# Opening loads on two queues, and bias transposes behind the first tile's last pair

## The reference

```
xn   = rms_norm(h, attn_norm_g[layer])          # per token over 1024 channels, times a gain
proj = xn @ w_in[layer]                         # 1024 x 2560: u_ssm, u_g, v_g, q, k, v
y_ssm  = s5_mixer(u_ssm, a_re, a_im, log_dt, b_re, b_im, c_re, c_im, d, w_glu, b_glu)
y_sgu  = spatial_gating(u_g, v_g, ...)
y_diff = diff_attention(q, k, v, ...)
h = h + concat(y_ssm, y_sgu, y_diff) @ w_out[layer]
h = h + conv_gated_mlp(rms_norm(h, ffn_norm_g[layer]), w_up, conv_w, conv_b, w_down)
```

## Time and profile before

| | |
|---|---|
| median of 3 runs | 967.36 us |
| profiled execution, its own time | 965.9 us |
| its span | 964.1 us |
| PE busy | 953.2 us (99%) |
| DVE, ACT, POOL busy | 71%, 59%, 24% |
| granted TensorE clock, mean | 0.999 |

### The profile page before, as it was taken

How to read it: one execution, slowest core, us unless ns; L and a number is a source line. 1 busy time by engine, 2 the same in 40 slices (tenths; PEclk the granted TensorE clock), 3 DMA queues, 4 the chain that set the end, 5 groups by cost and what they waited for, 6 DMA issues and landing times.

```text
span 964.1 us, 15784 instructions
## 1 busy us (share of the span) xinstructions
PE 953.2 (99%) x6119; PEld 837.0 (87%) x6123; DVE 687.8 (71%) x1081; ACT 567.4 (59%) x960; POOL 232.7 (24%) x189
## 2 busy tenths in 40 slices
PE   8999999999999999999999999999999999999997
PEld 6887889999888888899999988999778889888886
DVE  7987868786765877857777754748576755666885
ACT  7977666676855657756666544535454445555733
POOL 6560303535500110302445500021131300000030
PEclk9999999999999999999999999999999999999999
DMA  8642465655664534466665665665544445754452
GB/s 313 213 132 67 156 208 182 190 176 184 194 197 152 182 126 153 133 188 193 181 192 179 195 196 155 215 202 173 165 140 153 153 143 171 200 164 154 153 179 83
DMA packets 48618, 165.96 MB, mean 172 GB/s; under 512 B 6560, under 2 KB 7072, under 8 KB 48544
## 3 DMA queue, kind: packets, MB, share of 16 engines
q1 hardware_dynamic: 48544, 164.95, 54.3%
HBM read 162.83 MB, written 1.05 MB: 170 GB/s over the span
## 4 chain that ended last, share of the span: by engine, by line
PE 87%; ACT 4%; POOL 4%; DVE 3%; issue 1%; DMA 1%; SPq 0%; POOLq 0%; DVEq 0%; ACTq 0%
PE PJ L655 14%; PE PJ L657 13%; PE PJ L656 13%; PE PJ L648 10%; PE PJ L646 10%; PE PJ L647 10%; PE PJ L603 2%; PE PJ L586 2%; PE PJ L593 2%; PE T L1118 1%; ACT sm L1378 1%; ACT whi L1177 1%; PE T L1109 1%; DVE wlo L1874 1%; PE T L1047 1%
## 5 line engine op out<-in xcount | busy, mean ns | idle before, releaser
L1874 DVE TENSOR_TENSOR wlo<-raw,whi 128x1024 fp32r<-128x1024 f32 x294 | 368.7, 1284 | 87.0 <-ACT whi L1177 84.7
L1177 ACT ACTIVATE whi<-raw 128x1024 fp32r<-128x1024 f32 x294 | 301.8, 1059 | 62.9 <-DMA raw<-weights_in 60.6
L646 PE MATMUL PJ<-xthb,whi 128*128 128x256 f32 x832 | 233.7, 281 | 0.0
L648 PE MATMUL PJ<-xthb,wlo 128*128 128x256 f32 x832 | 233.4, 281 | 0.0
L647 PE MATMUL PJ<-xtlb,whi 128*128 128x256 f32 x832 | 232.4, 279 | 0.0
L655 PE MATMUL PJ<-whi,xthb 128*128 128x512 f32 (+1 forms) x424 | 170.9, 403 | 0.4 <-DVE wlo L1874 0.2
L657 PE MATMUL PJ<-whi,xtlb 128*128 128x512 f32 (+1 forms) x424 | 164.0, 387 | 0.0
L656 PE MATMUL PJ<-wlo,xthb 128*128 128x512 f32 (+1 forms) x424 | 163.9, 387 | 0.0
L647 PEld LDWEIGHTS PJ<-xtlb,whi 128*128 128x128 f32 x832 | 157.0, 189 | 0.3
L646 PEld LDWEIGHTS PJ<-xthb,whi 128*128 128x128 f32 x832 | 157.0, 189 | 0.3
L648 PEld LDWEIGHTS PJ<-xthb,wlo 128*128 128x128 f32 x832 | 156.9, 189 | 0.0
(11 more groups left out here) (419 smaller groups left out, 1353.8 us busy)
## 6 DMA issues: line engine op xcount, KB each, us to landing
raw<-weights_in SPq DMA_DIRECT2D x294, 512.0 KB, 3.6
rt<-bmerge_in SPq DMA_DIRECT2D x6, 256.0 KB, 4.2
memx<-mem_in SPq DMA_DIRECT2D x2, 512.0 KB, 4.2
y_out<-xn SPq DMA_DIRECT2D x4, 256.0 KB, 2.3
rowv<-rows_in SPq DMA_DIRECT2D x1, 576.0 KB, 10.4
xres<-x_in SPq DMA_DIRECT2D x2, 256.0 KB, 2.8
xres<-x_in SPq DMA_DIRECT2D x1, 512.0 KB, 6.7
ptmp<-bexp_in SPq DMA_DIRECT2D x2, 256.0 KB, 5.9
```

Source lines behind the costliest of these rows:

```text
L646: pe.matmul(o, a, xh[:, k, :], start=(first and f % 2 == 0), stop=False, skip_group_check=True)
L648: m = pe.matmul(o, b, xh[:, k, :], start=False, stop=last, skip_group_check=True)
L1177: act.activation(whi[:, p % HIGHS, :], raw[:, p % LOADS, :], ACT.Copy).then_inc(hi_ready, 1)
L1874: dve.tensor_tensor(wlo[:, p % LOADS, :], raw[:, p % LOADS, :], whi[:, p % HIGHS, :].bitcast(F32), ALU.subtract).then_inc(lo_ready, 1)
```

## The change

ACT issues two DMAs as its first instructions: the left half of tile 0's rows and weight pair 0. SP starts with the right half of tile 0's rows, then par and the identity, then pairs 1 and 2, tile 1's rows, pair 3, bex, pair 4 and the rest as before. On PE the four bias transposes stand behind pair j = 3 of tile 0 instead of j = 1. All other engines' lists, ACT's place of b_evac among them, stay as they are.

```diff
--- before.py
+++ after.py
@@ -438,17 +438,20 @@
                 sp.dma_start(dst, src).then_inc(sem(s), 16)
 
             n_par, n_id = COL["conv"][0], CST["ident"][1]
+
+            small(xres[:, 0, 512:1024], x[0:P, 512:1024], "x_landed0b")
             small(colv[:, 0:n_par], cols[:, 0:n_par], "par_landed")
-            for h in range(2):
-                small(xres[:, 0, 512 * h:512 * h + 512], x[0:P, 512 * h:512 * h + 512], f"x_landed0{'ab'[h]}")
             small(cst[:, 0:n_id], consts[:, 0:n_id], "ident_landed")
             for p, (nm, j) in enumerate(STREAM):
+                if p == 0:
+                    continue
                 if p >= LOADS:
 
                     sp.wait_ge(pair_used, p - LOADS + 1)
                 sp.dma_start(raw[:, p % LOADS, :], weights[FIRST[chunk(nm)] + j]).then_inc(raw_landed[p % LOADS], 16)
-                if p == 1:
+                if p == 2:
                     small(xres[:, 1, :], x[P:2 * P, :], "x_landed1")
+                if p == 3:
                     small(bexr, bexp[0], "bex_landed")
                 if p == 4:
                     small(cst[:, n_id:NCST], consts[:, n_id:NCST], "cst_landed")
@@ -893,7 +896,7 @@
                         pe.transpose(B[:, 1, 0:P], ident, ident)
                 for j in range(4):
                     tile_pairs(f"q{l}", 0, j, range(4), xth, xtl, ready=32 * l, upto=j + 1, weights_late=l == 0)
-                    if l == 0 and j == 1:
+                    if l == 0 and j == 3:
                         b_transposes(0, B[:, 0, :])
                     if j == 2:
                         norm_transposes(2 * l, (1,))
@@ -1259,6 +1262,8 @@
                     act.copy(mT[rows_, 4 * b:4 * b + 4, at_:P],
                              bank[rows_, :].rearrange("p (q n) -> p q n", q=4)[:, :, 0:P - at_]).then_inc(sem("mt_ready"), 1)
 
+            act.dma_start(xres[:, 0, 0:512], x[0:P, 0:512]).then_inc(sem("x_landed0a"), 16)
+            act.dma_start(raw[:, 0, :], weights[FIRST[chunk(STREAM[0][0])] + STREAM[0][1]]).then_inc(raw_landed[0], 16)
             act.wait_ge(sem("par_landed"), 16)
             act.activation(sp_[:, 0, :], col("ldt"), ACT.Exp).then_inc(sem("par_a"), 1)
             for half in range(2):
```

## The result

| | before | changed |
|---|---|---|
| median, 6 runs each | 967.14 us (966.19 to 967.41) | 970.75 us (970.27 to 971.08) |
| ratio | 1 | 1.0042, 95% interval 1.0032 to 1.0052 |
| profiled execution: its own time, span | 965.9, 964.1 | 970.27, 968.5 |

The change makes the kernel 3.6 us slower by the medians (3.1 to 5.0 by the interval); the two profiled executions differ by 4.4. The six executions of before include the three that were shown first. In the changed kernel ACT's and the later lines have moved by 3 to 5: L1268 is the old L1263, L1273 the old L1268, L1180 the weight's high part, L1216 b_evac, L1203 norm_hi.

What follows compares the result with a forecast made beforehand. TensorE, busy 99% of the span, was taken as the bound, delayed through ACT: 2.83 + 1.3 = 4.1 us takes the profiled 965.9 to 970.0; 1.46 more for the median gives 971.5, range 969.1 to 973.5.

Steps and rivals of the forecast that it cites:

- rival B: ACT catches up before 44 us, only PE's own delay counts: 1.77 + 1.3 = 3.1, so 970.5; chance 12%.
- rival E: Queues don't run side by side; ACT's table load precedes its issues, squares 0.8 late: 3.6, so 971.0; chance 6%.
- Late b_evac: ACT's b_evac waits for the moved transposes, so norm_hi of tile 1 starts at 20.20 instead of 17.37: 2.83 us late.
- Late parameters: Opening: par, queued behind half of the rows, lands at P = 4.6, so ACT's first weight starts 1.3 us late.
- s = P - 3.3: Delay s of ACT's first weight, from par's landing time P; taken as P = 4.6, s = 1.3 us.
- almost no slack: ACT up to the copy uT: whatever it is late at 17.37, it is late at 43.62, where PE waits 0.17 us.
- wrong if uT is less late than norm_hi: A sign named beforehand: the forecast is wrong if copy uT is delayed less than norm_hi of tile 1.
- PE to the end, nothing given back: After 44.27 PE stays late by the sum; its three named waits after 20 us come to 1.1 in all.
- The sentence said to carry most of the forecast: Whatever ACT is late at 17.37, it is late at 43.62, and PE has almost no slack there.
- A: Opening transfers are bound by latency, par hardly delayed: P = 3.1, sum 2.6, so 970.0; chance 15%.
- C: par shares the DMA engines with the first weight: P = 6.1, s = 2.8, sum 5.6, so 973.0; chance 11%.
- D: Not slower: the first weight was the bound, tile 0 starts 0.6 earlier, idle time hides b_evac: 966.8; chance 10%.

Runs made afterwards that it cites:

- par third: The changed kernel with the parameters one place further back in SP's queue, behind the identity: median 972.12 us, ratio 1.0058 to the kernel before.
- transposes only: The kernel before with the bias transposes behind pair 3 of tile 0, all loads as before: +2.5 us over before, ratio 1.0027.

## Why the prediction was right

It said 971.5, slower by 4.1, through two links in series. The median is 970.75, slower by 3.6. The time alone would not choose: 970.5 (rival B) and 971.0 (rival E) are nearer to it. What decides are the two links in the trace and the runs that take them one by one.

- *Late b_evac, 2.83:* measured 3.04 to 3.06 as the difference from the first weight to norm_hi. From the first bias transpose to ACT's start it took 21.24 - 20.37 = 0.87, where I had 0.69 from another group of transposes. ACT's wait for it, its place, and what stood behind were as told. PE's own delay by this link, forecast as 1.77, was 2.16: with the transposes only, PE's lows came 14.60 after the first weight's high part, before 12.44.
- *Late parameters, 1.3:* measured 1.61 between the two profiles, by P = 5.0 instead of 4.6. The row I took P from had the same bytes ahead of it, but in one queue. s = P - 3.3 held: 5.0 gives 1.7, and with par third one for one. The first weight landed at 6.0, where an earlier issue alone had been said to give 6.3; nothing hung on it.
- *ACT to uT, "almost no slack":* 0.37 of slack, seen in two kernels. I had the number in hand: 24.18 us less 23.72 busy is 0.46, small waits that no view lists singly, and I took them for nothing. By the prediction's own sign, "wrong if uT is less late than norm_hi", this part failed: 4.28 against 4.65. It is a small failure, as ACT kept nine tenths of its delay.
- *PE to the end, nothing given back:* 4.25 at the shuffle, 4.4 in the span. The sentence said to carry most of the forecast carried less than that: PE was 3.76 late at tile 1 by itself, and uT added 0.5.
- *Rivals.* A (par hardly delayed) falls with 5.02. B (ACT catches up) falls: ACT was still 4.28 late at uT, and where PE's own delay was only 1.6, PE waited for uT all the same. But with PE's own delay as measured B would have said 3.8 and not 3.1, only 0.5 under what happened. C's cause, a weight beside a small transfer, is seen (1.1 on the identity, 1.4 on par where both were first), but in the changed kernel it did not reach par. D and E fall: no weight was the bound, and the issues ran side by side from 0.72.
- *The remainder.* The terms as measured make 1.61 + 3.04 - 0.37 = 4.3, the profiles differ by 4.4, and the medians by 3.6. The kernels with SP's old order had their first weight's high part at 7.74, 8.20, 7.64 and 8.09, each after waiting for the DMA; the changed order had 9.35, 9.12 and 9.33, never waiting for it. The profile of before was an early one: the means, 7.92 and 9.27, give 1.35 for the first link and 4.0 in all. Part of what is left lies in the base: the forecast added 1.46 between the profiled execution of before and its median, and in the changed kernel the two lie 0.48 apart; against the 21 to 27 later executions of before (966.6 to 966.75) the change would be 4.0 to 4.15. Those were not taken beside it, so whether this is all stays open.

There was luck in the sum: an overlooked 0.37 stood against two terms that were 0.2 and 0.3 too small, so 4.1 came out beside 4.3.

## What to carry to other kernels

When work moves behind something, look first at who reads it and what stands behind that reader in its own queue; here four transposes that cost PE nothing held up a whole engine. An idle gap that hides an operation is used up by it: move the operation out, and it costs its full time wherever the engine has no gap. For a second DMA queue ask which landing the opening really waits for; the smallest transfer had the longest chain behind it and belonged first.

## What was not expected of the hardware

- A transfer at the head of its queue lands later when another queue has one beside it: par, 56 KB, issued at 0.72 in all of them, took 1.9 us with nothing on the other queue, 2.6 and 2.9 beside 256 KB of x with a weight behind it, and 3.3 beside a 512 KB weight.
- 64 KB of 512-byte rows took 3.4 us with no weight on the other queue and 4.5 with one, issued at the same time. Issued alone on ACT's queue at 2.63, beside the weights on SP's, they took 6.7.
- Two 256 KB halves on two queues land at 4.4 and 4.6; on one queue the first is there at 3.9 and the second at 4.5.
